# One pipeline for both attentions of layer 0, TensorE in rounds of two parts, and an earlier lo part of a token sum

## What is computed

```python
def forgetting_attention(q, k, v, log_f):        # per block of 128 queries
    s = einsum('bqhd,bkhd->bhqk', qb, k) * scale
    s = s + (cq[..., :, None] - cum[..., None, :])
    s = where(kpos[None, :] <= qpos[:, None], s, -inf)
    return einsum('bhqk,bkhd->bqhd', softmax(s), v)

def dsa_attention(q, k, v, qi, ki, wi, topk):    # per block of 128 queries
    _, sel = top_k(iscore, topk)                 # iscore: -inf behind the query's chunk
    s = einsum('bqhd,bqkd->bhqk', qb, gather(k, sel)) * scale
    return einsum('bhqk,bqkd->bqhd', softmax(s), gather(v, sel))

def conv_ffn(h, w_in, conv_w, conv_b, w_out):
    u = causal_depthwise_conv3(h @ w_in, conv_w) + conv_b
    gate, val = split(u, 2)
    return (gelu(gate) * val) @ w_out
```

## Time and profile before

| | us |
|---|---|
| median of 3 runs | 2371.26 (2368.92 to 2373.97) |
| the profiled execution: time | 2370.03 |
| its span, first to last instruction | 2367.5 |
| FoX, first to last matmul | 344.3 to 499.1 |
| DSA, first to last matmul | 506.3 to 639.8 |
| layer 0's round 0, product A22 starts | 831.6 |
| layer 1's round 0, product A22 starts | 1796.8 |

### The profile page before, as it was taken

How to read it: one execution, slowest core, us unless ns; L and a number is a source line. 1 busy time by engine, 2 the same in 40 slices (tenths; PEclk the granted TensorE clock), 3 DMA queues, 4 the chain that set the end, 5 groups by cost and what they waited for, 6 DMA issues and landing times. The chain is left out here.

```text
span 2367.5 us, 31632 instructions
## 1 busy us (share of the span) xinstructions
PE 2261.2 (96%) x11307; PEld 1906.0 (81%) x11307; DVE 1763.7 (74%) x2658; ACT 1194.2 (50%) x1968; POOL 847.2 (36%) x616
## 2 busy tenths in 40 slices
PE   6899979989999999999999989999999999999998
PEld 5678768889888878888878877888887888887886
DVE  4686677865554788888899866666577888889986
ACT  4457876766543434433444643555434443344454
POOL 2113213301010677788500002142157778870000
PEclk9999989999999999999999999999999999999999
DMA  5111100000152122222374442221222222228435
GB/s 152 42 31 51 39 19 28 28 2 1 40 175 80 50 87 87 81 83 87 124 259 133 152 151 74 64 71 55 82 79 78 84 80 86 84 80 280 151 119 188
DMA packets 190357, 215.15 MB, mean 91 GB/s; under 512 B 15508, under 2 KB 136692, under 8 KB 190204
## 3 DMA queue, kind: packets, MB, share of 16 engines
q1 hardware_dynamic: 185452, 195.84, 26.1%
q10 hardware_dynamic: 4752, 17.30, 1.8%
HBM read 170.77 MB, written 39.98 MB: 89 GB/s over the span
## 5 line engine op out<-in xcount | busy, mean ns | idle before, releaser
L122 PE MATMUL trunk_ps<-l_bhi,l_ahi 128*128 128x512 f32 x528 | 207.1, 392 | 4.8 <-DVE l_blo L2816 4.5
L122 PE MATMUL trunk_ps<-l_blo,l_ahi 128*128 128x512 f32 x528 | 206.3, 391 | 0.0
L122 PE MATMUL trunk_ps<-l_bhi,l_alo 128*128 128x512 f32 x528 | 206.2, 390 | 0.0
L122 PE MATMUL trunk_ps<-l_t_lo,l_s_hi 128*128 128x512 f32 x456 | 177.5, 389 | 0.0
L122 PE MATMUL trunk_ps<-l_t_hi,l_s_hi 128*128 128x512 f32 x456 | 177.5, 389 | 0.0
L122 PE MATMUL trunk_ps<-l_t_hi,l_s_lo 128*128 128x512 f32 x456 | 177.5, 389 | 0.0
L2444 POOL TENSOR_TENSOR l_s_lo<-l_raw,l_s_hi 128x512 fp32r<-128x512 f32 x90 | 160.5, 1791 | 42.7 <-ACT l_s_hi L2350 42.7
L2226 ACT ACTIVATE l_ahi<-l_a 128x512 fp32r<-128x512 f32 x132 | 83.0, 629 | 138.2 <-PE trunk_ps L122 135.2
L2444 POOL TENSOR_TENSOR l_s_lo<-l_w_sum,l_s_hi 128x512 fp32r<-128x512 f32 x76 | 120.0, 1582 | 48.1 <-ACT l_s_hi L2350 48.1
L214 POOL TENSOR_TENSOR wring_w_lo<-wring_raw,wring_w_hi 128x1024 fp32r<-128x1024 f32 x22 | 56.9, 2587 | 210.9 <-ACT wring_w_hi L210 210.9
L122 PEld LDWEIGHTS trunk_ps<-l_bhi,l_ahi 128*128 128x128 f32 x528 | 99.5, 188 | 29.4 <-DVE l_alo L2813 4.8
(11 more groups left out here) (472 smaller groups left out, 6715.2 us busy)
## 6 DMA issues: line engine op xcount, KB each, us to landing
l_draw<-in_ffn_w_out SPq DMA_DIRECT2D x154, 256.0 KB, 2.7
l_raw<-in_ffn_w_in SPq DMA_DIRECT2D x48, 512.0 KB, 4.5
gated_dram<-l_gate_out SPq DMA_DIRECT2D x44, 512.0 KB, 2.6
l_a<-gated_dram SPq DMA_DIRECT2D x88, 256.0 KB, 4.2
wring_raw<-in_even_w_in SPq DMA_DIRECT2D x20, 512.0 KB, 3.8
l_raw_g<-in_ffn_w_in SPq DMA_DIRECT2D x20, 512.0 KB, 3.9
l_raw_v<-in_ffn_w_in SPq DMA_DIRECT2D x20, 512.0 KB, 5.0
l_wt<-in_ffn_w_out SPq DMA_DIRECT2D x22, 256.0 KB, 5.7
```

The costliest lines, as they stand in the source:

```text
L122: mm = pe.matmul(o, w, m, start=a, stop=z, skip_group_check=onto)
```

## The change

Three things. (1) causal_stage is called once with 16 heads: the 64 steps of FoX, then the 64 of DSA, in one stage "mix" with 192 parts. DSA's query is packed like any head's; its key is packed by ScalarE right behind the hi parts of head 4 and by GpSimd behind the lo parts of head 4 (KEYS_AFTER), into a third key slot. Some buffers lie where the first heads' queries and keys were, so GpSimd and VectorE wait until those are packed (lo_packed). The chores stay spread over FoX's 96 parts, and VectorE waits for the last one ahead of DSA's first part. (2) TensorE's loop takes two parts per round: scores(p + 4), scores(p + 5), turn(p), turn(p + 1), values(p - 2), values(p - 1). (3) The lo part of t4 is made in four pieces of 512 elements ahead of gate(2), and the product A22 waits for one piece at a time.

The core of the diff:

```diff
@@ causal_stage, set-up
-    by_dve = [not forget and c > 0 for n, c, e in parts]
+    FOX_PARTS = first[TB * NH]
+    KEYS_AFTER = 4
+    fox = lambda n: steps[n]["h"] < NH
+    by_dve = [not fox(n) and c > 0 for n, c, e in parts]
...
+        k_lo.append(nc.alloc_sbuf_tensor_at("mix_k_lo2", [P, T], F32R, offset=spare[0]))
+        select.rank, select.eq = (nc.alloc_sbuf_tensor_at(f"mix_{x}", [P, T], F32, offset=at) for x, at in zip(("rank", "eq"), spare[1:]))
...
+        finishing = chores - 7 * select.nb
@@ causal_stage, GpSimd
                 for h in range(1, HEADS):
                     pack_head_lo(pool, h)
+                    if h == KEYS_AFTER:
+                        pool.wait_ge(key_hi, 2)
+                        for r in range(2):
+                            pool.tensor_tensor(k_lo[2][HD * r:HD * r + HD, :], dsa_keys, k_hi[2][HD:P, :].bitcast(F32), ALU.subtract).then_inc(key_lo, 1)
@@ causal_stage, TensorE
-                for j in range(AHEAD):
+                for j in range(AHEAD - 1):
                     scores(j)
-                for j in range(NPARTS + BEHIND):
-                    if j + AHEAD < NPARTS:
-                        scores(j + AHEAD)
-                    if j < NPARTS:
-                        turn(j)
-                    if j >= BEHIND:
-                        values(j - BEHIND)
+                for pair in range(0, NPARTS + BEHIND, 2):
+                    for j in range(pair, pair + 2):
+                        if j + AHEAD - 1 < NPARTS:
+                            scores(j + AHEAD - 1)
+                    for j in range(pair, pair + 2):
+                        if j < NPARTS:
+                            turn(j)
+                    for j in range(pair, pair + 2):
+                        if j >= BEHIND:
+                            values(j - BEHIND)
@@ causal_stage, ScalarE
-                for i in range(0 if keys is None else nkeys):
-                    for r in range(2):
-                        act.activation(k_hi[i][HD * r:HD * r + HD, :], keys[i], ACT.Copy).then_inc(key_hi, 1)
...
                     if j in packing:
                         pack_head_hi(act, packing[j])
+                        if packing[j] == KEYS_AFTER:
+                            for r in range(2):
+                                act.activation(k_hi[2][HD * r:HD * r + HD, :], dsa_keys, ACT.Copy).then_inc(key_hi, 1)
@@ causal_stage, VectorE
                 for j in range(NPARTS + AHEAD + BEHIND + 1):
+                    if j == FOX_PARTS:
+                        select.settle(dve)
                     if j < NPARTS:
                         bias_max(j)
-                    while select and j < NPARTS and chore < chores * (j + 1) // NPARTS:
+                    while j < FOX_PARTS and chore < chores * (j + 1) // FOX_PARTS:
+                        if chore == finishing:
+                            dve.wait_ge(lo_packed, 2)
                         select.late_chore(dve, chore, rounds)
                         chore += 1
@@ trunk_stage, TensorE
-                    if r == 0 and q == A22:
-                        pe.wait_ge(t4_lo_done, 1)
                     for k in range(QUARTER):
+                        if r == 0 and q == A22:
+                            pe.wait_ge(t4_lo_done, k + 1)
@@ trunk_stage, VectorE
                 taps("v", 2)
+                dve.wait_ge(t4_hi_done, 1)
+                for k in range(QUARTER):
+                    dve.tensor_tensor(t_lo[4][:, k, :], t4_sum[:, k, :], t_hi[4][:, k, :].bitcast(F32), ALU.subtract).then_inc(t4_lo_done, 1)
                 gate(2)
-                dve.wait_ge(t4_hi_done, 1)
-                dve.tensor_tensor(t_lo[4], t4_sum[:], t_hi[4].bitcast(F32), ALU.subtract).then_inc(t4_lo_done, 1)
-                dve.wait_ge(t4_lo_done, 1)
+                dve.wait_ge(t4_lo_done, QUARTER)
                 weight_sums(1)
```

More of the change, by code:

```diff
@@ L1546, in late_chore, with causal_stage @@
             self.finish(dve, b + 2, k)
-def causal_stage(nc, g, name, heads, keys, key_rows, steps, o_tm, forget=False, select=None, rounds=0):
+def causal_stage(nc, g, heads, dsa_keys, spare, steps, select, rounds):
     parts = [(n, c, min(x["nk"], c + HALF)) for n, x in enumerate(steps) for c in range(0, x["nk"], HALF)]
@@ L1627, in _ @@
             def _(sp):
-                for h in range(NH if forget else 0):
+                for h in range(NH):
                     if h >= 2:
@@ L1645, in scores @@
                         pe.wait_ge(lo_packed, h + 1)
[L1646 to L1648 removed]
+                    if j == FOX_PARTS:
+                        pe.wait_ge(key_lo, 2)
+                    if j == 0:
                         pe.wait_ge(mask_ready, 2)
```

64 lines of the change are left out of this document (24 added, 40 removed).

## The result

The change is slower: median 2376.62 us against 2369.83 us of the kernel before on the same chip, ratio 1.0024 with a 95% interval of 1.0014 to 1.0034, that is +5.7 us (+3.3 to +8.1). Two of the change's twelve executions were slow ones of 3231.68 and 4178.77 us at granted clocks of 0.652 and 0.801; they are in that median but not in the ratio, and the median of the other ten is 2374.7. The forecast was 2364.5. The profiled execution took 2374.69 us with a span of 2372.5.

A forecast was written before the change was run, and what follows sets the result against it. The prediction took TensorE, busy 96% of the span, as the bound. Pairing and fusion (-2.5 us) and the fourth sum (-4.3) made -6.8, from 2370.03 to 2363.2 profiled, forecast as a 2364.5 us median, range 2355 to 2377.

The follow-up runs named there:

- the kernel that lost 31 us: Kernel before with the fourth sum's lo part ahead of the gate, plus eight unneeded VectorE additions per layer ahead of merge(r): 2401.74 us, ratio 1.0143.

## What to carry to other kernels

A wait that ends earlier is a gain only if the engine that ends the stage comes earlier too. Follow the gain to the next place where TensorE waits for that engine, even if it is 350 us away, and ask in its list of waits whether the hurried engine occurs there; if it does not, it runs on its own time and the gain is only a lead. Two instructions' distance on the late engine, equal in two traces whatever TensorE does, points to it; but where the two engines' rounds are as near as 18.97 and 19.04 us, the distance hardly changes when the other engine takes over (358.6 and 358.0 here), and only the list of waits tells them apart. Work added to that engine tells how much slack it has, provided that it isn't put where the engine waits anyway.

And where two engines hand parts back and forth, taking two parts at a time halves the number of distances but moves each part's deadline up to the earlier one of the pair; look at each place that waits already.

## What the runs showed of the hardware

**VectorE beside GpSimd.** The same addition of two 128x512 operands from SBUF took 1.78 us where GpSimd worked beside it all the time (970.62, in the kernel that lost 31 us), 0.97 where GpSimd's subtraction ended within it (953.02), and 0.69 once where GpSimd stood still (1960.64, same kernel as 953.02); additions with one operand in PSUM took 0.67 to 0.69 in the same rounds. The Trainium skill (SBUF — State Buffer, section Who interferes with whom) says that a VectorE instruction with two SBUF inputs contends with a GpSimd instruction that reads SBUF, since its second input comes through an interface that they share; the rows agree with it. It made the added work twice as dear as I expected from the rows of 0.69.

**The slow stretches move.** With the same code, layer 1's front has them in different places and lengths. Windows of 1530 to 1555 before, in the change, with one part per round, and with the fourth sum and the weight sums moved:

```profile
1530.00:1555.00 25.00, 21.29 (x139) 18.90 (x138) 19.03 (x34) 16.32 (x44) 14.09 (x6) 0.86 0.81 206
```

```profile
1530.00:1555.00 25.00, 24.14 (x129) 22.33 (x128) 12.25 (x30) 15.59 (x40) 10.04 (x5) 0.66 0.87 218
```

```profile
1530.00:1555.00 25.00, 21.81 (x141) 19.32 (x139) 20.95 (x29) 17.04 (x41) 17.73 (x8) 0.93 0.57 156
```

```profile
1530.00:1555.00 25.00, 24.25 (x125) 22.48 (x126) 12.20 (x31) 15.04 (x40) 11.71 (x6) 0.66 0.80 206
```

Nothing that was changed here touches this stretch. From layer 0's down-projection to the fourth sum of layer 1 the single executions differ by up to 5.3 us, which is why differences of single traces were trusted only for waits and distances, and never for the end of the span. What decides where a slow stretch falls stays open.
